# Two transformer blocks on one core: attention scores of head pairs on the array's two row halves, with bias tiles added by VectorE

## Reference

```python
# layer 0 (one block of 256 keys, so every query sees its own block)
s_own = einsum('bhcd,bhkd->bhck', qc, k_own) * scale - slopes * dist_own     # slopes = 2 ** (-8 (h+1) / 16)
s_own = where(dist_own >= 0, s_own, NEG_INF);  out = softmax(s_own) @ v_own
# layer 1, c = cumsum(log_sigmoid(hn @ w_f + b_f))
sc = einsum('bhqd,bhkd->bhqk', qb, k) * scale + cq[..., None] - c[:, :, None, :]
sc = where(kpos <= tq, sc, NEG_INF);           out = softmax(sc) @ v
```

## Time and profile before

| | us |
|---|---|
| median of 3 runs (lowest, highest) | 1178.01 (1177.99, 1178.66) |
| profiled execution, its own time | 1178.95 |
| its span, first to last instruction | 1177.3 |
| PE busy | 1156.7 (98%) |
| DVE busy | 861.6 (73%) |
| ACT busy | 650.1 (55%) |
| POOL busy | 74.5 (6%) |
| TensorE clock granted | 0.998 of full speed |

### The profile page before, as it was taken

How to read it: one execution, slowest core, us unless ns; L and a number is a source line. 1 busy time by engine, 2 the same in 40 slices (tenths; PEclk the granted TensorE clock), 3 DMA queues, 4 the chain that set the end, 5 groups by cost and what they waited for, 6 DMA issues and landing times.

```text
span 1177.3 us, 17561 instructions
## 1 busy us (share of the span) xinstructions
PE 1156.7 (98%) x6735; PEld 1007.6 (86%) x6735; DVE 861.6 (73%) x1244; ACT 650.1 (55%) x896; POOL 74.5 (6%) x112
## 2 busy tenths in 40 slices
PE   9999999999999999999999999999999999999997
PEld 8897888888889888888878888888998888888886
DVE  6677798888867779988486665566986877655555
ACT  5555646655545555556565544456756765545453
POOL 9300011110000001110000000000000000000000
PEclk9999999999999999999999999999999999999999
DMA  8633699987463269997635665644651054655560
GB/s 275 218 138 119 224 335 351 329 309 259 147 193 132 73 215 347 344 333 260 214 108 182 212 212 180 191 155 148 197 185 67 33 191 135 215 193 200 167 208 36
DMA packets 143239, 236.33 MB, mean 201 GB/s; under 512 B 6357, under 2 KB 106950, under 8 KB 143174
## 3 DMA queue, kind: packets, MB, share of 16 engines
q1 hardware_dynamic: 130258, 196.47, 49.9%
q0 software_dynamic: 10400, 37.77, 8.7%
q10 hardware_dynamic: 2516, 1.22, 0.4%
HBM read 234.37 MB, written 1.05 MB: 200 GB/s over the span
## 4 chain that ended last, share of the span: by engine, by line
PE 86%; DVE 7%; ACT 3%; issue 2%; DMA 1%; POOL 0%; ACTq 0%; POOLq 0%; DVEq 0%
PE ps L2536 17%; PE ps L2539 9%; PE ps L2269 9%; PE ps L2271 9%; PE ps L2273 9%; PE ps L2224 5%; PE ps L2118 3%; PE ps L2126 3%; PE ps L2119 3%; DVE wlo L1226 2%; PE ps L2197 2%; PE ps L2198 2%; PE ps L2199 2%; PE ps L2375 1%; PE ps L2377 1%
## 5 line engine op out<-in xcount | busy, mean ns | idle before, releaser
L1226 DVE TENSOR_TENSOR wlo<-raw,whi 128x2048 fp32r<-128x2048 f32 (+2 forms) x180 | 404.8, 2260 | 128.4 <-ACT whi L651 127.7
L651 ACT ACTIVATE whi<-raw 128x2048 fp32r<-128x2048 f32 (+2 forms) x180 | 338.2, 1890 | 114.4 <-PE ps L2273 49.8
L2536 PE MATMUL ps<-a,whi 128*128 128x512 f32 x1024 | 255.8, 392 | 0.0
L2536 PEld LDWEIGHTS ps<-a,whi 128*128 128x128 f32 x1024 | 186.6, 188 | 35.5 <-issue 0.2
L2539 PEld LDWEIGHTS ps<-a,wlo 128*128 128x128 f32 x1024 | 139.7, 190 | 10.0
L2539 PE MATMUL ps<-a,wlo 128*128 128x256 f32 x1024 | 142.8, 282 | 0.0
L2269 PE MATMUL ps<-whi,hh 128*128 128x512 f32 x352 | 109.4, 392 | 0.8 <-DVE wlo L1226 0.8
L2271 PE MATMUL ps<-wlo,hh 128*128 128x512 f32 x352 | 108.7, 390 | 0.0
L2273 PE MATMUL ps<-whi,hl 128*128 128x512 f32 x352 | 108.5, 390 | 0.0
L1763 DVE SCALAR_TENSOR_TENSOR stage<-stage,cact 128x1024 f32<-128x1024 f32 x63 | 80.7, 1281 | 3.5 <-DMA stage<-in_w_ada_dram 1.9
L2271 PEld LDWEIGHTS ps<-wlo,hh 128*128 128x128 f32 x352 | 66.1, 188 | 14.3
(11 more groups left out here) (457 smaller groups left out, 2033.6 us busy)
## 6 DMA issues: line engine op xcount, KB each, us to landing
stage<-in_w_ada_dram POOLq DMA_DIRECT2D x72, 512.0 KB, 5.9
raw<-in_w_up_dram SPq DMA_DIRECT2D x32, 1024.0 KB, 7.2
raw<-in_w_down_dram SPq DMA_DIRECT2D x32, 1024.0 KB, 7.9
raw<-in_ffn_w_gate_dram SPq DMA_DIRECT2D x22, 1024.0 KB, 5.4
raw<-in_ffn_w_up_dram SPq DMA_DIRECT2D x22, 1024.0 KB, 5.4
raw<-in_ffn_w_down_dram SPq DMA_DIRECT2D x22, 1024.0 KB, 5.0
raw<-in_moba_w_qkv_dram SPq DMA_DIRECT2D x11, 1024.0 KB, 6.3
raw<-in_w_in_dram SPq DMA_DIRECT2D x10, 1024.0 KB, 5.0
```

What stands on the lines that cost most here:

```text
L651: A.activation(whi[:, s, 0:size], raw[:, s, 0:size], ACT.Copy).then_inc(w_hi, 1)
L1226: V.tensor_tensor(wlo[:, s, 0:size], raw[:, s, 0:size], whi[:, s, 0:size].bitcast(F32), ALU.subtract).then_inc(w_lo, 1)
L2536: T.matmul(bank(b + m), wh[:, c, m * P:(m + 1) * P], a2[:, c].rearrange("p k n -> p (k n)"), start=(c == 0), stop=False)
```

## The change

Queries and keys are stored with two heads of a pair on partitions 0 to 63 and 64 to 127 of one tile (`qx`, `kx` have H/2 tiles), so that a `qk_copy` is one instruction of 128 partitions. The bias row leaves the product. Instead each head has a bias tile of 128x384 (`bias`), mask included, which DVE's maximum adds in place of the mask tile; `p_max(h)` also waits for `bias_done`. In layer 0 POOL makes a base tile (iota, mask added) and scales it 16 times. In layer 1 DVE writes c twice into `rowf` (128 and 256 columns), SP sends each head's row to all 128 partitions of its tile by a DMA of its own, in five groups put between the weight loads (two groups behind load n0+8, one each behind n0+9, n0+10, n0+11), and POOL adds the mask to each tile. PE scores two heads together, the even one on rows 0 to 63 and the odd one on rows 64 to 127, each into its own bank; heads 14 and 15 are scored singly. The order on PE, ACT and DVE goes by pairs: PE runs two weights_T, the scores of the next pair, two fills, values. PE's waits for `krow_done` and `krow_landed` and POOL's copy are gone.

```diff
-        qx = st[:, 0:4096].rearrange("p (h n) -> p h n", h=H)
+        qx = st[:, 0:2048].rearrange("p (h n) -> p h n", h=H // 2)
-        kx = st[:, 6144:10240].rearrange("p (h n) -> p h n", h=H)
+        kx = st[:, 6144:8192].rearrange("p (h n) -> p h n", h=H // 2)
+        bias = ([st[:, 2048 + SEG * q:2048 + SEG * q + SEG] for q in range(5)]
...
+            def bias_rows(q):
+                sp.wait_ge(row_f, 1)
+                for h in range(*BIAS_GROUPS[q]):
+                    sp.dma_start(bias[h], rowf[h:h + 1].unsqueeze(1).to_broadcast([1, P, SEG])).then_inc(bias_landed[q], 16)
...
                     a_units(n0 + u, w, col + (m // 2) * AW, 1)
+                    if n0 == U_ATT1 and u > U_V + 4:
+                        if u == U_V + 5:
+                            bias_rows(0)
+                        bias_rows(u - U_V - 4)
...
+            def add_mask(tile):
+                return G.tensor_tensor(outer_blocks(tile), outer_blocks(tile),
+                                       maskv[:, P:S].unsqueeze(1).to_broadcast([P, 2, P]), ALU.add)
...
-            link(G.memset(qx[one], 1.0))
-            link(G.iota(kx[one], pattern=[[0, H], [1, S]], base=0, channel_multiplier=0,
+            base = bias[H - 1]
+            link(G.iota(base[:, 0:P], pattern=[[1, P]], base=0, channel_multiplier=0,
...
+            link(add_mask(base))
             for h in range(H):
-                G.tensor_scalar(kx[one, h], kx[one, h], slope * DH ** 0.5, None, ALU.mult).then_inc(krow_done, 1)
+                G.tensor_scalar(bias[h], base, slope * DH ** 0.5, None, ALU.mult).then_inc(bias_done, 1)
...
-            pool.wait_ge(row_f, 1)
-            pool.dma_start(kx[one].rearrange("p h n -> p (h n)"), rowf[0:H, 0:S]).then_inc(krow_landed, 16)
+            for q, (lo, hi) in enumerate(BIAS_GROUPS):
+                pool.wait_ge(bias_landed[q], 16 * (hi - lo))
+                for h in range(lo, hi):
+                    add_mask(bias[h]).then_inc(bias_done, 1)
...
-                for odd, heads_ in ((0, even_heads), (1, odd_heads)):
-                    r = rB[DH * odd:DH * odd + DH].unsqueeze(1).to_broadcast([DH, 2, S])
-                    ins = V.tensor_tensor(heads_(dst, quad), qk_half(m, odd), r, ALU.mult)
+                V.tensor_tensor(dst[:, 2 * quad:2 * quad + 2], by_c(bank(QK_BANK[m])),
+                                rB.unsqueeze(1).to_broadcast([P, 2, S]), ALU.mult).then_inc(qk_copied, 1)
...
                 def p_max(h):
+                    dve.wait_ge(bias_done, h0 + h + 1)
                     dve.wait_ge(scored, h0 + h + 1)
-                    head_max(h0 + h, h, bank(h % 2, SEG), scale)
+                    head_max(h0 + h, h, bank(h % 2, SEG), scale, bias[h])
...
+                for h in range(0, WOVEN, 2):
+                    p_max(h + 2)
+                    p_max(h + 3)
+                    splits(n0 + U_V + 6 + h // 2)
+                    normalise(h + 2)
+                    normalise(h + 3)
+                    if h % 4 == 0 and h:
+                        plain_part(h // 4 - 1)
+                    qk_copy(n0, 3 + h // 2)
...
+                for h in range(0, WOVEN, 2):
+                    weights_T(h)
+                    weights_T(h + 1)
+                    scores(h + 2)
+                    fill(h)
+                    fill(h + 1)
+                    values(h)
+                weights_T(10)
+                weights_T(11)
+                unit_wait(n0 + 12)
...
+                scores(12)
+                out_part(0, 0)
+                out_part(1, 0)
+                values(10)
+                score(14)
+                weights_T(12)
+                out_part(1, 1)
+                score(15)
+                weights_T(13)
+                out_part(2, 0)
+                values(12)
+                weights_T(14)
+                out_part(2, 1)
+                out_part(3, 0)
+                weights_T(15)
+                out_part(3, 1).then_inc(w_used, 1)
...
+            def head_score(h, cols, keys):
+                odd = h % 2
+                rows_ = slice(DH * odd, DH * odd + DH)
+                toks = slice(0, P) if cols.start == 0 else slice(P, S)
+                return T.matmul(bank(odd, SEG)[:, cols], qx[rows_, h // 2, toks], kx[rows_, h // 2, keys],
+                                start=True, stop=True)
+            def pair_scores(h):
+                for odd in range(2):
+                    head_score(h + odd, slice(0, P), slice(0, P))
+                for odd in range(2):
+                    head_score(h + odd, slice(P, SEG), slice(0, S)).then_inc(scored, 1)
...
-            V.tensor_scalar(rowf[0:H, 0:S], ps[0:H, 3, 0:S], -(DH ** 0.5), None, ALU.mult).then_inc(row_f, 1)
+            V.tensor_scalar(rowf[0:H, 0:P], ps[0:H, 3, 0:P], -(DH ** 0.5), None, ALU.mult)
+            V.tensor_scalar(rowf[0:H, P:SEG], ps[0:H, 3, 0:S], -(DH ** 0.5), None, ALU.mult).then_inc(row_f, 1)
```

More of the change, by code:

```diff
@@ L53 @@
 QK_BANK = [0, 1, 2, 6, 7, 6, 7, 6]
+BIAS_GROUPS = [(0, 2), (2, 4), (4, 8), (8, 12), (12, 16)]
 WOVEN = 10
@@ L258, in build @@
         scored = sem("scored")
-        krow_done = sem("krow_done")
-        krow_landed = sem("krow_landed")
+        bias_done = sem("bias_done")
+        bias_landed = [sem(f"bias_landed{q}") for q in range(len(BIAS_GROUPS))]
         p_normed = sem("p_normed")
@@ L902, in block_heads @@
                 tok_copy(att, 4, vt[:, 0])
-                for h in range(H):
-                    w_copy(h0 + h, h)
[L905 to L910, removed]
+                for h in range(0, WOVEN, 2):
+                    splits(n0 + U_V + 6 + h // 2)
+                    p_exp(h + 2)
+                    p_exp(h + 3)
+                    if h % 4 == 0 and h:
+                        plain(h0, h // 4 - 1, hh[:, h // 4 - 1])
+                    w_copy(h0 + h, h)
+                    w_copy(h0 + h + 1, h + 1)
+                w_copy(h0 + 10, 10)
+                w_copy(h0 + 11, 11)
+                p_exp(12)
+                p_exp(13)
+                w_copy(h0 + 12, 12)
+                p_exp(14)
+                w_copy(h0 + 13, 13)
+                p_exp(15)
+                w_copy(h0 + 14, 14)
+                plain(h0, 2, hh[:, 2])
+                w_copy(h0 + 15, 15)
                 splits(n0 + U_V + 11)
@@ L1423, in block_heads @@
                 normalise(0)
+                normalise(1)
                 tok_copy(att, 4, vt[:, 1])
-                for h in range(H):
-                    if h < WOVEN:
-                        normalise(h + 1)
-                    if h == WOVEN - 1:
-                        qk_copy(n0, 3 + h // 2)
-                    if h + 2 < H:
-                        p_max(h + 2)
-                    if h % 2 == 0 and h < WOVEN:
-                        splits(n0 + U_V + 6 + h // 2)
-                    if h % 2 == 1 and h < WOVEN - 1:
-                        qk_copy(n0, 3 + h // 2)
-                    if WOVEN <= h < H - 1:
-                        normalise(h + 1)
-                    if h >= 6 and h % 4 == 2:
-                        plain(stage_name, h // 4 - 1, hh[:, h // 4 - 1], hl[:, h // 4 - 1])
+                for h in range(0, WOVEN, 2):
+                    p_max(h + 2)
+                    p_max(h + 3)
+                    splits(n0 + U_V + 6 + h // 2)
+                    normalise(h + 2)
+                    normalise(h + 3)
+                    if h % 4 == 0 and h:
+                        plain_part(h // 4 - 1)
+                    qk_copy(n0, 3 + h // 2)
+                p_max(12)
+                p_max(13)
+                normalise(12)
+                p_max(14)
+                normalise(13)
+                p_max(15)
+                normalise(14)
+                normalise(15)
+                plain_part(2)
                 splits(n0 + U_V + 11)
@@ L2456, in block_heads, with out_part @@
-                values(H - 2)
-            def pair_score(h):
-                o = bank(h % 2, SEG)
-                q, k = qx[0:DH + 1, h], kx[0:DH + 1, h]
-                T.matmul(o[:, 0:P], q[:, 0:P], k[:, 0:P], start=True, stop=True)
-                return T.matmul(o[:, P:SEG], q[:, P:S], k, start=True, stop=True)
+                def out_part(c, t):
+                    if c % 2 == 0 and t == 0:
+                        pe.wait_ge(in_ready, PAIR0[stage_name] + c // 2 + 1)
+                    return wo_part(n0 + 12, t, 0, c, c == 0, False)
@@ new lines, in block_heads @@
+                scores(0)
+                d_unit(n0 + U_V + 3, slot(n0 + U_V + 3), 4, 2, D, ah, al, 6, False, True)
+                for h in range(0, WOVEN, 2):
+                    weights_T(h)
[7 more added lines that the diff above has]
+                unit_wait(n0 + 12)
+                pe.wait_ge(in_ready, PAIR0[stage_name] + 1)
```

78 lines of the change are left out of this document (27 added, 51 removed).

## The result

The changed kernel takes 1257.55 us (median of 4 runs, 1257.04 to 1258.1), the kernel before beside it 1178.24 us: 1.0672 times as long, 95% interval 1.0658 to 1.0685, or 79.3 us slower. The forecast was 1175.1 us, a gain, so it had the wrong sign, and the time lies above the range too (up to 1247). Rival 1 (1243.4 us) had the place and the mechanism and was 14 us short.

A forecast was written before the change was run, and what follows sets the result against it. PE, busy 98% of the span, was taken as the bound. Two layers at 1.4 us save 2.9 us, bias tiles and rows cost nothing: 1178.0 - 2.9 = 1175.1 us, range 1172.5 to 1247.

The forecast's parts named there:

- Rival 1: Second layer's bias rows: one source partition gives only 27.6 GB/s, 7.1 us a head, 1243.4 us in all; chance 0.32.
- Bias rows, second layer: 16 row DMAs on SP's queue run at full rate, 0.5 us each; load n0+9 still lands in time; cost nothing.
- the likeliest case: The forecast itself, with bias rows sent at full rate: 1175.1 us, own range 1172.5 to 1177.5; chance 0.45.
- Middle rates: Second layer's bias rows: loss starts near 1.7 us a head; at 3 us some 5 us lost, 1176 to 1195; chance 0.15.
- Score pairs: PE scores two heads on row halves at once: 0.95 us a pair, bounds 0.66 and 1.61, saving 0.37 each.
- Rival 2: PE's score pairs: row halves don't overlap, a pair costs 1.61 us, 1183.0 us in all; chance 0.05.
- Lone heads: Heads 14 and 15, scored singly on one half: 0.95 us instead of 0.66, a loss of 0.29 each.
- Start of a layer: PE waits for others there; fill(0) starts near 53.5 us instead of 52.67, yet the new order gains 0.15 us.
- The end of a layer: Last six heads: values end 14.6 us after fill(9), with no wait of more than 0.1 us.
- Sum of the pairs: Start of layer, five pairs and two lone heads together: 1.4 us gained per layer, 2.9 us over two.
- Bias tiles, first layer: GpSimd's 16 wider scalings take 1.3 us each plus hold-ups, bounds 0.84 and 4.1; ready before the maxima, cost nothing.
- Copy of queries and keys: One instruction of 128 partitions instead of two of 64 relieves DVE off the path, at no gain.

The follow-up runs named there:

- norows: Changed kernel with no bias row sent; GpSimd makes layer 1's tiles as in layer 0, without the forget bias: 1176.8 us, 0.9986 of before.
- spread16: Changed kernel with each head's row on eight partitions, 16 apart, all read by its DMA: 1178.41 us.
- port8: Changed kernel with each head's row on eight partitions, four apart, all read by its DMA: 1177.26 us, 0.9987 of before.
- adj8: Changed kernel with each head's row on eight neighbouring partitions, all read by its DMA: 1185.75 us, 1.0061 of before.
- poolq: Changed kernel with the 16 rows, each still from one partition, issued on GpSimd's queue instead of SP's: 1251.29 us, 1.0617 of before.
- serial: Kernel with rows on eight partitions four apart, but PE issuing a pair's heads one after the other: 1177.69 us, 0.9994 of before.

## Why the prediction was wrong, point by point

**Bias rows, second layer: the step that failed.** "At full rate (344 to 442 GB/s ...), 0.5 us a DMA", and from it "Cost nothing in this case". A row took 7.1 us, fourteen times as much, and norows shows that the whole loss hangs on these rows. The rate came from the weight loads of rows 8, which write 128 partitions; nothing in the trace of before reads one partition, and the text of rival 1 said so. The rate of the likeliest case was taken from the row that was nearest in bytes and not from the one that was nearest in shape. Rival 1 had priced the alternative: 442/16 = 27.6 GB/s, measured 26 or 27; 7.1 us a row, measured 7.1; start-up 3 us, measured 2.8.

**Rival 1, right mechanism, 14 us short.** Its dates are for row_f at 341.5, measured 339.9. Group 0 was due at 358.7 and came at 356.9, group 1 at 372.9 (371.1), group 2 at 403.9 (398.9), group 4 at 465.9 (456.7); the rows were in fact a few us early. The term that was wrong is what remains after that: 11.4 us behind the maximum of head 12. The rival's queue ended with load n0+11, yet load n0+12 stands behind group 4 too, and ACT needs it for a pair much earlier than head 12. From 460.03 on 29.7 us remained to the end of the values (489.7) in place of 11.4. Part of it is the lower clock: from the values of heads 6 and 7 (464.36) to the next fill (468.70) PE took 4.3 us (granted clock 0.63 in the mean of 464 to 470 us), and 2.5 for the same steps in layer 0 (59.49 to 61.95). The rival followed the delay to the loads between the groups and not to the one behind them. With layer 0's 1.4 us, which it takes off last, its values end at 476.4: 13.3 of the 14 us lie there, and 0.8 behind the heads.

**Middle rates.** "It decides from about 1.7 us a head on" is about right: at 1.6 us (spread16) ACT waits 1.3 us for load n0+9 and up to 5.6 for the next, and 1178.4 us is already 1.6 above norows; at 1.1 (port8) ACT waits for no load. "At 3 us a head some 5 us are lost" was too little: at 3.3 (adj8) 9 us are lost against norows.

**Score pairs.** Taken 0.95 us, bounds 0.66 and 1.61. With values, transposes and fills at the prices of the forecast (0.95, 0.66, 5.74) the 8.39 us measured leave 1.04 for the pair. Right mechanism, 0.09 us too cheap a border. Rival 2 (1.61 us) is out.

**Lone heads.** Taken 0.95. In the changed kernel values(10) starts at 97.80 and values(12) at 102.65. Of these 4.85 us, values, two weights_T and two output parts at the prices of the forecast take 0.95, 0.66 and 1.36, which leaves 0.94 for each lone head: as forecast.

**Start of a layer.** fill(0) forecast near 53.5, measured 53.54.

**The end of a layer.** Forecast 14.6 us from the end of fill(9) to the end of the values. In the changed kernel values(8) starts at 93.06 and the last values end about 107.8: 14.8.

**Sum of the pairs.** Forecast 1.4 us a layer; measured 1.2 and 1.0, in all 2.2 us at the end of the heads and 1.7 in the medians of norows, where the forecast had 2.9. Even had the rows been free, the gain would have been below the 2.4 us that the forecast held to be measurable; the interval of norows (0.9976 to 0.9995) just leaves out no gain.

**Bias tiles, first layer.** Taken 1.3 us plus hold-ups; measured 1.17 at the shortest and 3.22 at the longest. The last starts at 35.3, and the head that needs it is scored at 100.63. Cost nothing, as forecast. The mask of a tile costs GpSimd 0.70 us, inside 0.25 to 2.0.

```profile
L626 POOL TENSOR_SCALAR stage<-work x12: 1169/1178/3017, 6.5 to 32.3; 128x384 f32<-128x384 f32 x12
L626 POOL TENSOR_SCALAR work<-work x4: 1172/2184/3217, 23.2 to 35.3; 128x384 f32<-128x384 f32 x4
```

**Copy of queries and keys.** One instruction instead of two, no cost on the path, as forecast.

## What to carry to other kernels

A transfer is priced by the partitions that it touches (here those it reads; no run tried few on the writing side), not by its bytes: the same 197 KB took 7.1 us from one partition or from four neighbours, and 1.1 us from eight that lie four apart. When the trace has no transfer of that shape, the case at the low rate belongs in the sum as an equal. A slow transfer must be followed to everything behind it that uses the same DMA engines, also on other queues and also behind its last part. And where one row has to reach all partitions, copies of it made by the operation that computes it (here by a matmul with more output rows; port8 lies 0.5 us above norows) or a trip through DRAM (2.9 us for two rows, 1178.17 us in all) avoid the limit.

## What the runs showed of the hardware

- One partition, or four neighbouring ones, give a DMA 27 to 30 GB/s, whether 4 or 16 engines read. The engines count as busy meanwhile: a busy share of 0.88 came with 30 GB/s. Only share and GB/s together show the fault.
- SP's issue instruction is itself held up by a slow stream. An issue of a weight load that takes 0.37 us took 7.3, 13.4 and 7.3 us behind the rows (the rows of L455 above), so that later loads are also issued late. In poolq, with the rows on GpSimd's queue, SP's issues took 0.38 and 0.37 us while rows were in flight. That SP's queue had no room is my reading.
- The engines are shared across queues: a slow stream on GpSimd's queue left SP's loads 3.1% of the engines' time. The Trainium skill, DMA: Bandwidth & Descriptors, Queues, rings and completion order, has each engine take turns between its queues a packet at a time; the rows of poolq agree: 444 packets of the slow queue and 527 of SP's went in the same 49 us, a turn of the slow queue being long.
- Matmuls on the two row halves overlap in either order of issue: 0.86 us for a pair in port8 and in serial, where a single head's scores took 0.66.
- The granted clock fell to 0.73 of full speed in the mean of 350 to 400 us, where PE was busy less than half of the time, between its two levels of 1.2 and 2.4 GHz, and the page shows it back at full speed from slice 16 on. The lower level came with the starvation and is not its cause: PE waited for ACT's copies there, and ACT for loads. The row is the busy time of the changed kernel in that stretch.

```profile
350.00:400.00 50.00, 21.89 (x139) 18.16 (x137) 10.64 (x38) 7.09 (x20) 3.90 (x6) 0.73 0.89 65
```
